# Three reorderings in a six-layer fp32 transformer kernel: pooled low halves, a row sum, and the turn for rotary keys

## The chip, the cores and the metric

The kernel runs on one core of a Trainium2 chip. The metric is the device time of one execution in microseconds; the figure for the kernel before is the median of three runs. Positions in the trace ("at 263 us") count from the first instruction of the profiled execution.

## What is computed

One sequence of 512 tokens with 1024 features passes through a pool mixer, a gated convolution, a latent attention with 16 heads, a second pool mixer, and then two layers that each hold a mixed attention and a feed-forward part. All is float32. The parts that the change touches:

```python
# pool mixer: u, z = split(xn @ w_in); 4 groups g with window w = 2, 4, 8, 16
mean = (c - prev) / min(count, w)          # trailing mean of u, c = cumsum(u)
pooled = mean - u
mixed = (pooled @ w_grp[g]) * scale
x = x + (mixed * silu(z)) @ w_out
# latent attention, per head
q, kv = rms_norm(q_lat) @ w_q_up, rms_norm(kv_lat) @ w_kv_up
p = softmax((q_nope @ k_nope + rope(q_rope) @ k_rope) * scale, causal)
o = p @ v;  x = x + (o * silu(z)) @ w_out
# feed-forward
h = rms_norm(x);  x = x + square(relu(h @ w_ff1)) @ w_ff2
```

## The kernel before

Activations lie transposed in SBUF: 8 tiles x[m] of 128 features by 512 tokens. Every float32 operand of a product is split into a high half (rounded to fp32r) and a low half (the rest), and a product is three matmuls: high by high, high by low, low by high (`mm3`, lines 401 to 404). All weights come in units of up to 128 by 1024, in one fixed order. A unit passes through four hands: SyncE loads it into one of 4 raw buffers, ScalarE writes its high half wh (line 875), VectorE (line 1448) or GpSimd (line 2173) writes its low half wl, and TensorE multiplies it, as a rule with 8 tiles of activations, so 24 matmuls (`xgemm`, `gemm8`). There are only 3 wh and 3 wl buffers. `taking(unit)` on an engine stands for "make the halves of all units up to this one plus two".

The normalisation is not applied to x before the product. The squares of x are summed while the products run already (ScalarE squares, GpSimd adds into acc, line 2182), TensorE sums acc over the partitions by a product with ones (`sum_squares`, line 428), ScalarE takes the root (906), VectorE the reciprocal (1464), and the results of the products are multiplied by it when they are taken out of PSUM (`scaled`, line 1474, or line 2121 in the feed-forward part).

Each engine has a queue written out by hand, which it works through in order. The places that matter:

- `pool_layer` (TensorE 449, ScalarE 954, VectorE 1513). A group g has four u tiles, four z tiles, two units of the group's product. VectorE works on a u tile like this: low half of the weight unit two ahead, take the product out of PSUM (1474), g+1 shifted adds (1530), mean minus token (1535), two fixes of the first columns (1537, 1540), and then the low half of the pooled tile into G (`low`, 1456), which needs the high half. ScalarE has in its queue, for each u tile: high half of the pooled tile (884), then the high half of the next weight unit (875).
- `mla_layer`, the latent attention (TensorE 502 on, ScalarE 1025 on, VectorE 1658 on, GpSimd 2234 on). Even heads bring the rotary part for themselves and the next head: ScalarE copies it with its rows swapped, VectorE multiplies by cos (1614), GpSimd multiplies the swapped copy by sin (2189) and adds (2192, the tile t1; this is `turn`), ScalarE takes the high halves (1035, 1036), VectorE the low halves (1677, 1678), and TensorE uses them in the rotary part of the scores (550). GpSimd also scales the exponentials of each head to probabilities in four instructions (`probs`, 2240), which TensorE transposes behind the next head's scores (490).
- `second_layer`, the feed-forward part: `first_pair` runs the first two weight units, then `sum_squares`, then the units from the third on; ScalarE, VectorE and GpSimd have relu, square and both halves of their results in their queues behind the root. PSUM banks are handed out from a ring (`bank`).

Of the kernel before, what the change touches and what calls it, by code (L numbers as in the profile page):

```python
# [275 lines left out]
def program(nc, D, out):  # L276
    ctx = ExitStack()
    with ctx:
# [101 lines left out]
        def pe_program(handle, c):  # L380
# [36 lines left out]
            def xgemm(st, *key, first=False):  # L417
                gemm8(key, XH, XL, (lambda k: ("xl", st, k)) if first else None)
# [5 lines left out]
            def sum_squares(use):  # L424
                b = bank("rs", use)
                pe.wait_ge(*at(*last_square(use)))
                pe.wait_ge(*at("const"))
                pe.do.matmul(b[:, :], ones, ACC[:, :], start=True, stop=True).then_inc(  # L428
                    *mark("group", ("mm", "rs", use), ("accfree", use)))
# [203 lines left out]
            def second_layer(l):  # L633
# [165 lines left out]
                wo(1, 3, (3,)), wo(1, 5), wo(1, 7), wo(1, 6)  # L799
                first_pair()  # L800
                ring[0] = [home[i] for i in LAST_BANKS]
                sum_squares(st + 1)
                for qd in range(4):
                    for i in range(2 if qd == 0 else 0, 8):
                        xgemm(st + 1, "f1", l, qd, i)
                    if l == 1 and qd == 3:
                        last_proj()
                    else:
                        out_proj(f"f2{l}", qd)
# [46 lines left out]
        def act_program(handle, c):  # L856
# [21 lines left out]
            def taking(*key):  # L878
                weights(unit[key] + LOOK)
# [145 lines left out]
            def mla_layer(done):  # L1025
# [4 lines left out]
                def rope_high(h):  # L1030
                    t = temp("t1", "m", h)
                    act.wait_ge(*at("t1", "m", h))
                    if h:
                        act.wait_ge(*at("mm", "sc", h - 1, 34))
                    act.do.activation(RQ[0][0:64, :], t[0:64, :], ACT.Copy)
                    act.do.activation(RQ[1][64:128, :], t[64:128, :], ACT.Copy).then_inc(*mark("act", ("rqh", h)))
# [47 lines left out]
                high(KRH[:, :], temp("t1", "m", "kr"), ("t1", "m", "kr"), ("rqh", "kr"))  # L1084
                taking("mz", 0)
                rope_high(0)
                silu(0)
                taking("ke", 0)
                k_high(0)
                for h in range(15):  # L1090
                    if h:
                        turned(h - 1)
# [330 lines left out]
        def dve_program(handle, c):  # L1423
# [27 lines left out]
            def taking(*key):  # L1451
                weights(unit[key] + LOOK)
# [59 lines left out]

            def pool_layer(j, st, out_st):
                sc_name = f"pool_scale{j}"
                for g in range(4):
                    w = 2 ** (g + 1)
                    for i in range(4):
                        taking("u", j, g, i)
                        if g == 0 and i == 0:
                            recip_root(st, R[:, :])  # L1520
                        key = (j, g, i)
                        U = own_temp(dve, at, "U", *key)
                        scaled(U, st, ("u",) + key)
                        dve.wait_ge(*at("pads"))
                        src, names = ("U",) + key, ("B1", "B2")
                        for d in range(g + 1):
                            dst = (names[d % 2],) + key
                            o = own_temp(dve, at, *dst)
                            dve.wait_ge(*mine())
                            dve.do.tensor_tensor(o, temp(*src), shifted(src, 2 ** d), ALU.add).then_inc(*mark("dve"))  # L1530
                            src = dst
                        other = own_temp(dve, at, names[(g + 1) % 2], *key)
                        s = temp(*src)
                        dve.wait_ge(*mine())
                        dve.do.scalar_tensor_tensor(other, s, 1.0 / w, U, ALU.mult, ALU.subtract).then_inc(*mark("dve"))
                        dve.wait_ge(*mine())
                        dve.do.tensor_tensor(other[:, 0:w], s[:, 0:w], const[:, C_CNT + 16 * g:C_CNT + 16 * g + w],
                                             ALU.mult).then_inc(*mark("dve"))
                        dve.wait_ge(*mine())
                        dve.do.tensor_tensor(other[:, 0:w], other[:, 0:w], U[:, 0:w], ALU.subtract).then_inc(  # L1540
                            *mark("dve", ("pooled",) + key, ("tfree", "U") + key))
                        k = (g % 2) * 8 + i
                        low(G[k + 4][:, :], other, G[k][:, :], ("gh",) + key, ("gl",) + key, ("tfree", "B1") + key,
                            ("tfree", "B2") + key)
                    for i in range(4):
                        taking("z", j, g, i)
                        scaled(PZ[i], st, ("z", j, g, i), ("zr", j, g, i))
                    for i2 in range(2):
                        taking("grp", j, g, i2)
                        for i in (2 * i2, 2 * i2 + 1):  # L1550
                            key = (j, g, i)
                            t = own_temp(dve, at, "gy", *key)
                            dve.wait_ge(*at("mm", "grp", *key))
                            dve.wait_ge(*at("zs", *key))
                            dve.do.scalar_tensor_tensor(t, ps("grp", *key)[:, :], vcol(sc_name, 4 * g + i), PZ[i],
                                                        ALU.mult, ALU.mult).then_inc(
                                *mark("dve", ("gy",) + key, ("psfree", "grp") + key))
                            yi = (g % 2) * 4 + i
                            low(YL[yi][:, :], t, YH[yi][:, :], ("yh", f"po{j}", g // 2, yi),
                                ("yl", f"po{j}", g // 2, yi), ("tfree", "gy") + key)  # L1560
                    if g % 2:
                        out_proj(f"po{j}", g // 2, out_st if g == 3 else None)
# [95 lines left out]
            def mla_layer():  # L1658
# [75 lines left out]
                q_low(0)  # L1734
                low(KRL[:, :], temp("t1", "m", "kr"), KRH[:, :], ("rqh", "kr"), ("rql", "kr"), ("tfree", "t1", "m", "kr"))
                taking("mz", 0)
                gate(0)
                rope_low(0)
                taking("ke", 0)
                k_low(0)  # L1740
                for h in range(15):
                    scores(h)
                    if h:
# [404 lines left out]
        def pool_program(handle, c):  # L2148
# [85 lines left out]
            def mla_layer():  # L2234
# [19 lines left out]
                for h in range(15):  # L2254
                    if h % 2:
                        taking("qe", h + 1)
                        probs(h)
                        turn(("m", h + 1))
                        taking("ke", h + 1)
                        taking("mz", h + 1)  # L2260
                    else:
                        taking("mz", h + 1)
                        probs(h)
                        taking("qo", h)
                        taking("vk", h)
                    if h == 8:
                        out_proj("mo", 0)
# [299 lines left out]
```

## Time and profile before

| | |
|---|---|
| median of three runs | 2791.34 us (2783.97 to 2792.09) |
| the profiled execution: its time, its span | 2790.05 us, 2788.3 us |
| TensorE (PE) busy | 2719.6 us, 98% of the span |
| VectorE (DVE) busy | 1560.8 us, 56% |
| ScalarE (ACT) busy | 1138.8 us, 41% |
| GpSimd (POOL) busy | 634.2 us, 23% |
| DMA | 238.78 MB, mean 86 GB/s |
| granted TensorE clock, mean | 0.991 |

The profile names a group of instructions by its line, engine and operation and by out<-in. "Idle before" is the time that an engine stood still ahead of an instruction, with what released it. A matmul of 512 columns shows 0.39 us, but starts follow each other closer, as they are pipelined.

### The profile page before, as it was taken

What the parts mean: (1) busy time and instruction counts of PE and PEld (TensorE: products, weight loads), DVE (VectorE), ACT (ScalarE), POOL (GpSimd) and SP (SyncE); (2) the same over time, 40 slices, a digit from 0 to 9 for tenths busy, and PEclk for the clock granted to TensorE, in tenths of its full rate; (3) what the DMA queues carried; (4) which work ended last, traced back from release to release, by engine and by line L of the source; (5) the groups of instructions that cost most, each with busy time, mean ns of one, the idle gap of its engine ahead of it and who ended that gap; (6) DMA issues with size and microseconds to landing.
All of it is one profiled execution on the core that took longest, in us unless ns stands there. A gap on an engine that the chain in (4) does not pass through costs nothing.

```text
span 2788.3 us, 32068 instructions
## 1 busy us (share of the span) xinstructions
PE 2719.6 (98%) x12958; PEld 2271.4 (81%) x12958; DVE 1560.8 (56%) x2306; ACT 1138.8 (41%) x1826; POOL 634.2 (23%) x418
## 2 busy tenths in 40 slices
PE   7999999999989999999999999999999999999998
PEld 6887888888878888888878888778888888788887
DVE  6656555344565646566565768644435668644433
ACT  4313432222345636533225767522224667522222
POOL 1000111011125625400003651411102452411101
PEclk9999999999999999999999999999999999999999
DMA  3222323223221121222222221133333211233231
GB/s 136 98 91 91 101 97 100 98 91 105 92 65 55 58 82 63 76 99 98 91 96 96 76 70 37 61 99 98 95 96 107 76 61 46 61 98 98 92 105 68
DMA packets 68836, 238.78 MB, mean 86 GB/s; under 512 B 7632, under 2 KB 10192, under 8 KB 68688
## 3 DMA queue, kind: packets, MB, share of 16 engines
q1 hardware_dynamic: 68688, 236.73, 26.3%
q8 instruction: 102, 1.67, 0.2%
q14 instruction: 46, 0.38, 0.0%
HBM read 234.60 MB, written 2.10 MB: 85 GB/s over the span
## 4 chain that ended last, share of the span: by engine, by line
PE 84%; DVE 7%; POOL 4%; ACT 3%; issue 1%; DMA 0%; POOLq 0%; SPq 0%; DVEq 0%; ACTq 0%
PE ps L402 27%; PE ps L404 26%; PE ps L403 26%; DVE t L1530 1%; ACT wh L875 1%; POOL s L2240 1%; POOL acc L2182 1%; DVE wl L1448 1%; PE ps L704 1%; PE ps L703 1%; PE ps L490 1%; PE ps L428 1%; POOL wl L2173 1%; DVE xl L1460 1%; DVE t L1474 0%
## 5 line engine op out<-in xcount | busy, mean ns | idle before, releaser
L402 PE MATMUL ps<-xh,wh 128*128 128x512 f32 x1936 | 766.0, 396 | 19.4 <-DVE wl L1448 10.8
L404 PE MATMUL ps<-xh,wl 128*128 128x512 f32 x1936 | 756.9, 391 | 0.0
L403 PE MATMUL ps<-xl,wh 128*128 128x512 f32 x1936 | 756.9, 391 | 0.0
L875 ACT ACTIVATE wh<-raw 128x1024 fp32r<-128x1024 f32 (+2 forms) x453 | 463.5, 1024 | 448.0 <-PE ps L404 447.5
L1448 DVE TENSOR_TENSOR wl<-raw,wh 128x1024 fp32r<-128x1024 f32 (+1 forms) x337 | 412.3, 1224 | 150.8 <-ACT wh L875 150.8
L402 PE MATMUL ps<-yh,wh 128*128 128x512 f32 x1152 | 450.0, 391 | 1.9 <-DVE wl L1448 1.6
L402 PEld LDWEIGHTS ps<-xh,wh 128*128 128x128 f32 x1936 | 365.6, 189 | 104.5 <-DVE wl L1448 20.9
L403 PE MATMUL ps<-yl,wh 128*128 128x512 f32 x1152 | 448.3, 389 | 0.0
L404 PE MATMUL ps<-yh,wl 128*128 128x512 f32 x1152 | 448.3, 389 | 0.0
L403 PEld LDWEIGHTS ps<-xl,wh 128*128 128x128 f32 x1936 | 365.9, 189 | 77.9 <-issue 3.2
L404 PEld LDWEIGHTS ps<-xh,wl 128*128 128x128 f32 x1936 | 365.4, 189 | 77.0
L2173 POOL TENSOR_TENSOR wl<-raw,wh 128x1024 fp32r<-128x1024 f32 (+3 forms) x116 | 258.4, 2237 | 428.1 <-ACT wh L875 427.9
L2182 POOL TENSOR_TENSOR acc<-acc,t 128x512 f32<-128x512 f32 x66 | 89.5, 1356 | 794.7 <-ACT t L896 792.7
L1482 DVE TENSOR_TENSOR x<-ps,x 128x512 f32<-128x512 f32 x160 | 109.9, 689 | 276.5 <-PE ps L404 276.5
L402 PEld LDWEIGHTS ps<-yh,wh 128*128 128x128 f32 x1152 | 216.3, 188 | 47.6 <-DVE wl L1448 2.0
L404 PEld LDWEIGHTS ps<-yh,wl 128*128 128x128 f32 x1152 | 216.2, 188 | 45.2
L403 PEld LDWEIGHTS ps<-yl,wh 128*128 128x128 f32 x1152 | 216.3, 188 | 44.2
L884 ACT ACTIVATE yh<-t 128x512 fp32r<-128x512 f32 x148 | 93.2, 631 | 365.4 <-POOL t L2356 252.2
L1456 DVE TENSOR_TENSOR yl<-t,yh 128x512 fp32r<-128x512 f32 x148 | 122.2, 827 | 193.2 <-ACT yh L884 193.2
L2356 POOL TENSOR_TENSOR t<-t 128x512 f32<-128x512 f32 x64 | 66.7, 1042 | 531.7 <-DVE t L2121 531.7
L1460 DVE SCALAR_TENSOR_TENSOR xl<-x,vec,xh 128x512 fp32r<-128x512 f32 x64 | 88.7, 1403 | 63.9 <-ACT xh L886 63.9
L884 ACT ACTIVATE g<-t 128x512 fp32r<-128x512 f32 x45 | 28.3, 628 | 179.0 <-DVE t L1540 175.3
(233 smaller groups left out, 3547.7 us busy)
## 6 DMA issues: line engine op xcount, KB each, us to landing
raw<-in_ff SPq DMA_DIRECT2D x128, 512.0 KB, 3.6
raw<-in_pool_in SPq DMA_DIRECT2D x64, 512.0 KB, 3.3
raw<-in_conv_in SPq DMA_DIRECT2D x64, 512.0 KB, 3.2
raw<-in_pool_out SPq DMA_DIRECT2D x32, 512.0 KB, 3.2
raw<-in_qk SPq DMA_DIRECT2D x32, 512.0 KB, 3.6
raw<-in_pool_grp SPq DMA_DIRECT2D x16, 512.0 KB, 3.3
raw<-in_conv_out SPq DMA_DIRECT2D x16, 512.0 KB, 3.3
raw<-in_mla_z SPq DMA_DIRECT2D x16, 512.0 KB, 3.5
```

The source lines that it names most:

```text
L402: pe.do.matmul(o, lh, rh_, start=start, stop=False)
L403: pe.do.matmul(o, lh, rl_, start=False, stop=False)
L404: return pe.do.matmul(o, ll, rh_, start=False, stop=stop)
L875: act.do.activation(h[:, 0:ncol], r[:, 0:ncol], ACT.Copy).then_inc(*mark("whi", ("whi", k)))
L884: act.do.activation(dst, src, ACT.Copy).then_inc(*mark("act", done))
L1448: dve.do.tensor_tensor(lo[:, 0:ncol], r[:, 0:ncol], f(h[:, 0:ncol]), ALU.subtract).then_inc(*mark("wlo", ("wlo", k)))
L1456: dve.do.tensor_tensor(dst, src, f(h), ALU.subtract).then_inc(*mark("dve", *done))
L1460: dve.do.scalar_tensor_tensor(dst, src, scale, f(h), ALU.mult, ALU.subtract).then_inc(*mark("dve", *done))
L1482: dve.do.tensor_tensor(x[m][:, :], ps(*key)[:, :], x[m][:, :], ALU.add).then_inc(*mark("dve", ("psfree",) + key, *done))
L2173: pool.do.tensor_tensor(lo[:, 0:ncol], r[:, 0:ncol], f(h[:, 0:ncol]), ALU.subtract).then_inc(*mark("wlop", ("wlo", k)))
L2182: pool.do.tensor_tensor(ACC[:, :], ACC[:, :], temp("sq", use, k), ALU.add).then_inc(*mark("pool", ("acc", use, k), ("tfree", "sq", use, k)))
L2356: pool.do.tensor_tensor(t, t, t, ALU.mult).then_inc(*mark("pool", ("ffs",) + key))
```

## The change

1. VectorE, pool mixer: the low half of the pooled tile i is no longer taken at the end of its own tile but in the next tile, between `scaled` and the shifted adds; that of the fourth tile comes behind `scaled` of the first z tile. ScalarE's queue there is the same as before.
2. TensorE, feed-forward part of both later layers: `sum_squares` stands behind the third weight unit rather than ahead of it. With it the two swap their PSUM banks.
3. Latent attention. GpSimd, odd heads: `turn` and the low half of the weight unit that `taking("ke")` stands for come ahead of `probs`. ScalarE and VectorE, before the first head: the high and low half of the first keys come ahead of the gate's silu and scaling.

```diff
@@ second_layer, TensorE @@
                 first_pair()
                 ring[0] = [home[i] for i in LAST_BANKS]
-                sum_squares(st + 1)
                 for qd in range(4):
                     for i in range(2 if qd == 0 else 0, 8):
                         xgemm(st + 1, "f1", l, qd, i)
+                        if qd == 0 and i == 2:
+                            sum_squares(st + 1)
@@ mla_layer, ScalarE @@
                 rope_high(0)
+                k_high(0)
+                taking("ke", 0)
                 silu(0)
-                taking("ke", 0)
-                k_high(0)
@@ pool_layer, VectorE @@
+                def pooled_low(g, i, src):
+                    key, k = (j, g, i), (g % 2) * 8 + i
+                    low(G[k + 4][:, :], src, G[k][:, :], ("gh",) + key, ("gl",) + key, ("tfree", "B1") + key,
+                        ("tfree", "B2") + key)
...
                         scaled(U, st, ("u",) + key)
+                        if i:
+                            pooled_low(g, i - 1, last)
                         dve.wait_ge(*at("pads"))
...
-                        k = (g % 2) * 8 + i
-                        low(G[k + 4][:, :], other, G[k][:, :], ("gh",) + key, ("gl",) + key, ("tfree", "B1") + key,
-                            ("tfree", "B2") + key)
+                        last = other
                     for i in range(4):
                         taking("z", j, g, i)
                         scaled(PZ[i], st, ("z", j, g, i), ("zr", j, g, i))
+                        if i == 0:
+                            pooled_low(g, 3, last)
@@ mla_layer, VectorE @@
                 taking("mz", 0)
+                rope_low(0)
+                k_low(0)
                 gate(0)
-                rope_low(0)
                 taking("ke", 0)
-                k_low(0)
@@ mla_layer, GpSimd @@
                     if h % 2:
                         taking("qe", h + 1)
-                        probs(h)
                         turn(("m", h + 1))
                         taking("ke", h + 1)
+                        probs(h)
                         taking("mz", h + 1)
```

## Rows read from the trace of the kernel before

**Rows 1.** Waits of TensorE: us in total, times, longest us.
```profile
PE ps L402 <- DVE wl L1448: 12.4, 11, 1.9
PE ps L550 <- DVE g L1678: 8.2, 7, 1.2
```

**Rows 2.** Timeline, DVE, a u tile of g = 3: start, us, [idle before].
```profile
259.94 0.17 DVE L1540 TENSOR_TENSOR t<-t 128x16 f32<-128x16 f32 x1
260.81 0.69 DVE L1456 TENSOR_TENSOR g<-t,g 128x512 fp32r<-128x512 f32 x1 [0.70 <-ACT g L884]
261.76 1.23 DVE L1448 TENSOR_TENSOR wl<-raw,wh 128x1024 fp32r<-128x1024 f32 x1 [0.26 <-ACT wh L875]
```

**Rows 3.** Timeline, DVE, outputs of two units in a row in an output projection.
```profile
157.68 0.69 DVE L1482 TENSOR_TENSOR x<-ps,x 128x512 f32<-128x512 f32 x1 [3.06 <-PE ps L404]
...
163.12 0.69 DVE L1482 TENSOR_TENSOR x<-ps,x 128x512 f32<-128x512 f32 x1 [3.06 <-PE ps L404]
```

**Rows 4.** Timeline, PE, first matmuls of units in g = 2 and g = 3.
```profile
212.50 0.50 PE L402 MATMUL ps<-xh,wh 128*128 128x512 f32 x1 [0.46 <-DVE wl L1448]
...
263.04 0.50 PE L402 MATMUL ps<-xh,wh 128*128 128x512 f32 x1 [1.28 <-DVE wl L1448]
...
270.64 0.50 PE L402 MATMUL ps<-xh,wh 128*128 128x512 f32 x1 [1.84 <-DVE wl L1448]
```

**Rows 5.** Timeline, PE and DVE, g = 0: the fourth u unit, and a wl three units later.
```profile
43.07 0.50 PE L402 MATMUL ps<-xh,wh 128*128 128x512 f32 x1 [0.30 <-DVE wl L1448]
...
57.97 1.23 DVE L1448 TENSOR_TENSOR wl<-raw,wh 128x1024 fp32r<-128x1024 f32 x1 [0.26 <-ACT wh L875]
```

**Rows 6.** Timeline, POOL, odd head 1.
```profile
853.23 2.41 POOL L2173 TENSOR_TENSOR wl<-raw,wh 128x1024 fp32r<-128x1024 f32 x1 [8.52 <-ACT wh L875]
855.62 4.28 POOL L2240 TENSOR_SCALAR s<-s,small 128x128 f32<-128x128 f32 x4
...
862.56 3.81 POOL L2173 TENSOR_TENSOR wl<-raw,wh 128x1024 fp32r<-128x1024 f32 x2
```

**Rows 7.** Timeline, DVE, same head.
```profile
857.72 0.69 DVE L1614 TENSOR_TENSOR t<-ps,cos 128x512 f32<-128x512 f32 x1 [2.33 <-ACT t L1008]
...
863.94 1.57 DVE L1677 TENSOR_TENSOR g<-t,g 64x512 fp32r<-64x512 f32 x1 [3.54 <-ACT g L1036]
865.52 1.39 DVE L1678 TENSOR_TENSOR g<-t,g 64x512 fp32r<-64x512 f32 x1
866.94 0.69 DVE L1474 TENSOR_TENSOR s<-ps,r 128x512 f32<-128x512 f32 x1
867.55 0.68 DVE L1709 TENSOR_TENSOR t<-ps,s 128x512 f32<-128x512 f32 x1
868.93 0.69 DVE L1456 TENSOR_TENSOR yl<-t,yh 128x512 fp32r<-128x512 f32 x1 [0.70 <-ACT yh L884]
```

**Rows 8.** Timeline, PE: first transposition of head 1's probabilities.
```profile
868.70 0.27 PE L490 MATMUL ps<-const,s 128*128 128x128 f32 x1
```

**Rows 9.** Timeline, DVE and PE, before the first head.
```profile
825.93 1.97 DVE L1677 TENSOR_TENSOR g<-t,g 64x512 fp32r<-64x512 f32 x1 [0.19 <-ACT g L1036]
...
829.56 0.77 PE L402 MATMUL ps<-g 128*128 128x512 f32 x1 [5.20 <-DVE g L1456]
```

**Rows 10.** Timeline, PE and ACT, feed-forward start of the first later layer.
```profile
1801.10 2.08 PE L428 MATMUL ps<-acc,const 128*128 128x512 f32 x2 [4.36 <-POOL acc L2182]
...
1803.26 1.28 ACT L906 ACT_TABLE_LOAD   x1 [6.25 <-PE ps L428]
...
1816.62 0.50 PE L402 MATMUL ps<-xh,wh 128*128 128x512 f32 x1 [1.89 <-DVE wl L1448]
```

**Rows 11.** Windows: from:to, length, busy of PE, PEld, DVE, ACT, POOL, granted clock, DMA.
```profile
829.50:835.00 5.50, 5.44 (x19) 5.18 (x20) 0.69 (x4) 1.27 (x1) 1.82 (x1) 0.50 0.62 188
1818.10:1821.40 3.30, 3.30 (x9) 2.57 (x8) 2.17 (x3) 1.58 (x2) 0.18 (x1) 0.50 0.34 132
2446.60:2449.50 2.90, 2.90 (x13) 2.41 (x14) 1.08 (x2) 1.22 (x2) 1.04 (x1) 1.00 0.54 177
```

## The prediction

> **What bounds the kernel now.** First the page: TensorE is busy 98% of the span, so the other engines matter only where TensorE waits for them. Then the list of its waits [rows 1]: the two heads shown are low halves of weight units that VectorE delivers late (12.4 us) and the rotary low half in seven heads (8.2 us); two more waits appear in the timelines, 5.20 us before the first head of latent attention [rows 9] and 4.36 us at the feed-forward row sum [rows 10]. The change aims at such gaps, so what counts is what ends each of them and what is queued behind it. A unit of 24 matmuls takes 5.44 us at full clock: in an output projection VectorE takes one product each 163.12 - 157.68 us, waiting for TensorE both times [rows 3].
>
> **Pooled low halves: +10.5 us.** In group g = 3 the unit starts at 263.04 and 270.64 each had to wait for a wl [rows 4], 7.60 us apart, against 5.44 us of work: the engines that prepare set the pace, and each tile's lateness reaches TensorE in full once its lead is used up. What is on that chain? After the last fix of a tile ends at 260.11, VectorE waits 0.70 us for ScalarE's high half g, takes the low half from 260.81 to 261.50, waits 0.26 us more, and starts wl at 261.76, released by ScalarE's wh [rows 2]. ScalarE's queue holds g first and wh behind it, and g needs the finished tile. So the 1.65 us from 260.11 to 261.76 belong to ScalarE, and the low half lies inside them for nothing. Moved away, it leaves an idle VectorE there; wl starts no earlier. Put in between `scaled` and the adds, it stands on the chain: VectorE is not waiting there. It costs one slot of a 128x512 operation, 867.55 - 866.94 = 0.61 us [rows 7], say 0.60, in each tile but the first. The fourth low half falls behind `scaled` of the first z tile, where VectorE waits for ScalarE again, and costs nothing.
>
> So the wl's of the first, second and third z unit, made in the course of these tiles, come 0.6, 1.2 and 1.8 us later; the second and third are those at 263.04 and 270.64, the third is the last to bind, and TensorE is 3 x 0.60 = 1.8 us later from there on. In the z tiles the chain is shorter than 5.44 us, so the lateness is not given back and not increased: a group costs 1.8 us less its slack at that unit. By group:
> - g = 3: it waits already, slack 0, +1.8 us.
> - g = 2: it waits too (0.46 us at 212.50) [rows 4], slack 0, +1.8 us.
> - g = 1: each tile has one add less, 0.73 us; over four tiles the 0.5 us of g = 2 become a slack of about 2.4 us. More than 1.8: nothing.
> - g = 0: TensorE starts its fourth u unit at 43.07, late; three units on it needs a wl at 43.07 + 3 x 5.44 = 59.39, and that one is there at 57.97 + 1.23 = 59.20 [rows 5]. Its late start has used up the lead of a group that is otherwise fast. With 0.05 us to react the slack is 0.15, so 1.8 - 0.15 = 1.65 us.
>
> A layer: 1.65 + 0 + 1.8 + 1.8 = 5.25 us, two layers 10.5 us. The ends: were `scaled` and low half to overlap fully the cost would be 0; with 0.69 us for a slot it is 12. I take 0.61 as the only row of two such operations back to back. No DMA and no other queue moves; GpSimd is idle there.
>
> **Row sum one unit later: +2.4 us.** Before, TensorE stands 4.36 us until 1801.10 and 1.89 us until 1816.62 [rows 10]. The unit that now goes first has its halves and fills the first gap. But the second gap is released by a wl that stands in VectorE's queue behind the reciprocal and two feed-forward tiles, which all need the row sum; ScalarE's wh of that unit is behind two of its high halves as well. What does the sum itself do? The third unit runs from about 1796.6 to 1802.0, then come the two passes at full clock, about 1.1 us, and ScalarE's root can begin at 1803.15 in place of 1803.26. So the fifth unit starts some 0.1 us earlier, and the 4.4 us filled come out again ahead of it: the fourth unit ends at 1808.8, and TensorE stands until 1816.5, about 7.7 us in one piece. Twice, this gains 0.2 us. And one long gap has a price: after the 5.20 us of [rows 9] the granted clock was 0.50, which is 1.2 of 2.4 GHz, for the next 5.5 us [rows 11], which loses half of that, 2.7 us. The gaps of before cost less behind the fifth unit's start: 0.50 for 3.3 us in the first later layer, and 1.00 in the second [rows 11], 1.65 us together. With 3.3 to 5.5 us at half speed in each layer the cost is 3.3 to 5.5, middle 4.3, less 1.65, less 0.2: +2.4 us, ends +1.4 and +3.6, and -0.2 if no stretch at half clock follows.
>
> **Turn ahead of probabilities: -3.1 us.** In head 1 the turn waits for `probs` to end at 855.62 + 4.28 = 859.90 [rows 6]; its input, the swapped copy, is there at 857.7 [rows 7]. So it moves up by 2.2 us, line 1677 is issued at 861.75 instead of 863.94, and TensorE's wait of 1.2 us [rows 1] goes. What is late next is `probs`, pushed behind turn (2.66 us) and one wl (2.41 us) [rows 6]: wl ends at 862.8, four instructions on their own end at 862.8 + 4.28 = 867.1. Without the wait TensorE asks for them at 868.70 - 1.2 = 867.5 [rows 8]. That would fit. But VectorE and GpSimd are not independent here: lines 1677 and 1678 took 1.57 and 1.39 us beside the wl's of GpSimd [rows 6, 7], where a 128x512 operation takes 0.69, and the second wl, of 384 columns, came out at the end of them. Each such meeting with lines 1677 and 1678 delays `probs` by about 0.4 us, since they take 0.55 us of the shared turn and the instruction had begun: 867.9. The low half of y is issued 2.0 us behind line 1678 [rows 7], hence at 866.35, just as the fourth instruction of `probs` begins; if it gets in first, 0.6 us more: 868.5. So the transposition starts at 867.95 or 868.55 in place of 868.70, 0.75 or 0.15 us gained, in seven heads 5.2 or 1.0. I take the middle, 3.1; the ends are 0 and 8.2.
>
> The Trainium skill ("SBUF — State Buffer", Who interferes with whom) states that a VectorE instruction with two SBUF inputs and a GpSimd instruction that reads SBUF exclude each other, whoever issues first holding the ports for its whole length. The 1.57 us of [rows 7] agree. By its rule the fourth instruction, which begins 0.03 us ahead of the low half of y, would win, and the part would be -5.2 rather than -3.1.
>
> **First keys ahead of the gate: +0.4 us.** ScalarE's k_high comes 1.8 us earlier, but VectorE's k_low stands behind lines 1677 and 1678, and 1677 took 1.97 us beside a wl of GpSimd [rows 9]. It ends at 827.9 as before. And now ScalarE's next wh is earlier too, so GpSimd has its wl of 384 columns waiting when 1677 ends, and 1678 meets it as in head 1: 1.39 us, not 0.69. k_low ends near 829.9 where it ended at 829.5. Ends: -0.3 without that meeting, +0.5. The gate's tile and silu, moved behind, have 5 us until exponentials are due.
>
> **Sum.** 10.5 + 2.4 - 3.1 + 0.4 = +10.2 us on the profiled execution's 2790.05, so 2800.2. The median of the three runs lies 1.3 us higher; carried to it: 2801.5. About 0.3% (8.4 us) is what a measurement of this kernel can tell from no change.
>
> **The rivals.**
> - *Attention gives all it can.* `probs` ends before 867.5 in spite of the meetings: -8.2 instead of -3.1, in sum +5.1, 2796.6 us. For it: the GpSimd instructions are short. Against: 1.57 and 1.39.
> - *More stretches at half clock.* The z units of g = 3 then wait 2.6 and 2.0 us, the one of g = 2 about 2.0 where it was 0.5. Each stretch like that of 1818.10 [rows 11] costs 1.65; with two to three more, +14 to +15, 2806 us. Against: a stretch ahead of another wait for VectorE is absorbed in it.
> - *Faster: the tile's cycle gets shorter.* If wh does not have to wait for g, the 0.70 + 0.26 us of idle VectorE per tile [rows 2] go and the low half only fills: the cycle falls from 7.60 to 6.6 us, and the waits of the low weight halves, 7.2 us of them in the two pool layers, vanish, with half-clock stretches of some 3 us. With the rest of the sum, 2.4 - 3.1 + 0.4 = -0.3, that is about -10.3: 2781 us. It decides where ScalarE's wh would start before the tile is finished. Against it: the row's releaser, wh 1.65 us behind the tile, and a ScalarE queue that the change leaves alone.
> - *The lows cost nothing*, but nothing is gained either: 2791 us.
>
> **How the numbers follow.** My forecast 0.60, attention in full 0.14, more half clock 0.13, faster 0.06, lows free 0.07. Of the forecast's own range (+6 to +13.5) a fifth lies under 8.4 us: slower 0.48 + 0.13 = 0.61, same 0.12 + 0.14 + 0.07 = 0.33, faster 0.06. The range leaves out faster and half of lows free: 2793 to 2809.
>
> **What would show it.** In the profile after: in g = 2 and 3 an idle VectorE of about 1.65 us before each u tile's wl, and 8.2 us between the wl's in g = 3; waits for wl at TensorE up from 12.4 to some 22 us. A wait of 7 to 8 us ahead of the fifth feed-forward unit, with wl as its releaser, and hardly one at the sum. Line 550 without a wait, line 490 with one of 0.4 to 1.1 us on GpSimd in seven heads. Before the first head still 5.5 us. I am wrong if wh starts ahead of g, if the fifth unit starts more than 1 us earlier, or if no wait appears at line 490.

## The result, and the profile after

| | before | after |
|---|---|---|
| median of seven runs each, same chip | 2790.20 us (2783.97 to 2792.29) | 2798.18 us (2796.05 to 2799.39) |
| ratio, 95% interval | | 1.0035 [1.0026, 1.0044] |
| profiled execution: time, span | 2790.05 us, 2788.3 us | 2797.78 us, 2796.0 us |

The kernel became slower by 0.35%, 9.8 us (0.0035 x 2790). The forecast was +10.2 us, so the sign, the size and the range held. The profiled executions, both at a mean granted clock of 0.991, lie 7.7 us apart. How much of the forecast is understanding shows only part by part. The lines named below moved: one further for ScalarE's and VectorE's helpers (wl is now line 1449, the low half 1457, `scaled` 1475), nine further for GpSimd's (wl 2182, `probs` 2249) and for VectorE's rotary lines (1686, 1687).

TensorE's waits in the profile after (us in total, times, longest us), to be held against [rows 1]:

```profile
PE ps L402 <- DVE wl L1449: 31.6, 19, 7.2
...
PE ps L402 <- DVE g L1457: 5.8, 1, 5.8
...
PE ps L490 <- POOL s L2249: 5.4, 7, 0.8
```

Late low halves of weight units cost 31.6 us where they cost 12.4. Of the 31.6, 14.4 are two waits of 7.2 us, one in each feed-forward part, where before had 3.1 us; the other 17.2 stand against 9.3 us of before, and all that is new in them is in the pool mixers, 15.6 us against 7.7. The wait at line 550 (8.2 us in seven heads) is gone, and one at line 490 on GpSimd's probabilities has come, 5.4 us in the same seven heads.

Since the order of TensorE's work hardly changed, the two traces can be laid side by side by the number of the matmul, and the lag of one against the other read at each stage (a later start than in the kernel before counts as positive). That reading is worked out from the starts of all matmuls and has no row of its own. It is taken where the lag has settled, behind any stretch at half clock:

| stage | lag gained there | forecast |
|---|---|---|
| start-up, up to the first units | -1.2 us | 0 |
| pool mixer 1: g = 0, 1, 2, 3 | +1.6, 0, +1.8, +1.8 | +1.65, 0, +1.8, +1.8 |
| before the first head | +0.2 | +0.4 |
| seven odd heads | 7 x -0.38 = -2.7 | -3.1 |
| pool mixer 2: g = 0, 1, 2, 3 | +1.6, 0, +1.8, +1.8 | +1.65, 0, +1.8, +1.8 |
| a stretch at half clock near 1699 us of before, absent after | -0.6 | 0 |
| feed-forward, first and second later layer | +1.1, +1.3 | +2.4 together |
| end | -0.8 | 0 |
| total | +7.7 (as the spans) | +10.2 |

So every part has the forecast sign, and none misses by more than 0.5 us; the stages that the change touches add up to +10.3. The 2.5 us between +7.7 and +10.2 are start-up, end and the missing stretch near 1699 us, which the change does not touch. The timed +9.8 lies nearer to the forecast than the profiled pair, and part of that is the clock: all seven executions of the kernel after have a mean granted clock of 0.991, while those of the kernel before in the experiments below range from 0.991 (2788.7 to 2793.5 us) to 0.994 (2783.5 to 2786.3 us).

### The profile page after: what moved, and what is told of

Same layout as the page of the kernel before. It is cut to its first block, busy times and chain, and to the rows that moved or that the text cites. A ratio compares the mean times of both kernels' runs of the same rounds, so it can differ in the third digit from the quotient of the medians.

```text
span 2796.0 us, 32057 instructions
## 1 busy us (share of the span) xinstructions
PE 2717.7 (97%) x12958; PEld 2265.6 (81%) x12958; DVE 1554.6 (56%) x2306; ACT 1141.2 (41%) x1826; POOL 639.1 (23%) x418
## 4 chain that ended last, share of the span: by engine, by line
PE 84%; DVE 7%; ACT 4%; POOL 3%; issue 1%; DMA 0%; SPq 0%; POOLq 0%; DVEq 0%; ACTq 0%
PE ps L402 27%; PE ps L403 26%; PE ps L404 26%; POOL s L2249 1%; ACT wh L876 1%; DVE t L1539 1%; DVE wl L1449 1%; ACT t L1009 1%; PE ps L490 1%; PE ps L704 1%; PE ps L703 1%; DVE g L1457 1%; POOL wl L2182 1%; PE ps L428 1%; DVE t L1475 1%
```

## The experiments

Each kernel was timed beside the kernel before on one chip; ratios carry a 95% interval, and us are the ratio's distance from 1 times some 2787 us.

### Theory and rivals

The theory is that of the prediction: four independent parts; the low halves used to lie inside VectorE's idle time behind ScalarE's queue and now lie on the chain; the row sum turns a pair of gaps into one long gap; `turn` ahead of `probs` trades one wait for a shorter one. The rivals are that the loss comes from granted clock and not from the moved work, that the pool part costs also where there is slack, and that ScalarE's order, not VectorE's load, is what holds the pool layers.

### Each part alone

Only the pooled low halves (part 1 of the diff).

> Only the pooled low halves are moved, the rest is as before. My theory (the low half lay for nothing inside VectorE's wait for ScalarE's wh, and now stands on the chain): TensorE loses about 1.5, 0, 1.9 and 1.8 us in the groups g = 0 to 3 of each pool layer, 10.4 us in all, ratio near 1.0037; VectorE is idle 1.65 us ahead of each u tile's wl. Rival (the lows cost nothing and the loss of the change comes from elsewhere): no step in TensorE's times in the pool layers, ratio 1.000.

Measured: 1.0042 [1.003, 1.0055], +11.7 us. TensorE's wait for wl in this kernel (lines as in before):

```profile
PE ps L402 <- DVE wl L1448: 17.4, 19, 2.5
```

From 12.4 to 17.4 us, and at the start of the last late unit of each group the matmul-by-matmul lag has stepped by 1.6, 0, 1.8 and 1.8 us, in both layers: 10.4 us. Not all of it stays in this execution. Its half-clock stretch comes one unit earlier than in before, between the two waits of g = 3 (from:to, length, busy of PE, PEld, DVE, ACT, POOL, granted clock, DMA share, GB/s):

```profile
266.80:270.10 3.30, 3.30 (x8) 2.62 (x9) 3.13 (x5) 0.00 (x0) 0.00 (x0) 0.50 0.49 159
```

There the second wait swallows it (0.87 us are left of the 2.46 of the kernel after), while the stretch of before lies behind that unit and costs 1.6 us. Settled, g = 3 therefore costs 0.2 us here, and the two layers 7.2 us. The spans differ by 8.8 us, 3.1 us of which come from one more half-clock stretch near 1752 us of before (last section). So the timed +11.7 is not the moved instruction alone: all five executions have a mean granted clock of 0.991, the 21 of the kernel before have a median of 0.993, and beside those of them at 0.991 (2789.0 to 2791.7 us) this kernel (2797.6 to 2799.3 us) is some 8 us slower. By this estimate the rival of the granted clock holds for 3 to 4 us of the timed figure; the steps show the rest. This part carries the loss of the whole change.

Only the row sum (part 2).

> Only the feed-forward row sum is moved behind the third unit. My theory (the fifth unit's wl hangs on the sum, so the filled gap comes out again, in one piece, and is followed by more time at half clock): a wait of about 7.2 us ahead of the fifth unit in both layers, that unit starts within 0.3 us of where it did, and TensorE is 0.5 to 2 us later behind it in each layer: +1 to +4 us, ratio 1.0004 to 1.0014. Rival (the filled gap is a gain that something else in the change hides): -4 us or more in each layer, ratio 0.997 or less.

Measured: 1.0018 [1.0009, 1.0027], +5.0 us with ends of 2.5 and 7.5. Waits, fifth unit, and two windows behind it (columns as above), one in each later layer:

```profile
PE ps L402 <- DVE wl L1449: 23.8, 11, 7.2
```

```profile
1815.13 0.79 PE L402 MATMUL ps<-xh,wh 128*128 128x512 f32 x1 [7.25 <-DVE wl L1449]
```

```profile
1815.20:1820.00 4.80, 4.80 (x12) 3.73 (x13) 2.73 (x4) 1.58 (x2) 1.04 (x1) 0.50 0.38 109
2445.70:2451.00 5.30, 5.30 (x13) 4.14 (x14) 2.93 (x4) 1.58 (x2) 1.26 (x2) 0.50 0.28 99
```

One wait of 7.25 us, and behind it 4.8 and 5.3 us at half clock, where before had 3.3 us and none [rows 11]. By matmuls the part costs 0.5 us in the first layer, which had a half-clock stretch of its own, and 2.6 us in the second. That is 3.1 us, near the forecast (2.4) and inside the timed interval, whose middle is higher. One likely reason is that the stretch of 3.3 us in before is not always there (the profiles of the third and fourth experiment have none at that place), while those of 4.8 and 5.3 us stand behind waits of 7.2 us; the mean granted clock is 0.991 (median of 11 executions) beside 0.993. How much of the 5.0 us that explains was not measured.

Only GpSimd's order in the odd heads (part 3 without the first keys).

> Only GpSimd's turn and one low half are moved ahead of the probabilities in the odd heads. My theory (the wait at the rotary scores goes, and one of 0.76 us at the transpositions takes its place): 0.41 us gained in each of seven heads, -2.9 us, ratio 0.9990. Rival (the waits are exchanged one for one): 0 us, ratio 1.0000.

Measured: 0.9985 [0.9976, 0.9994], -4.2 us; by matmuls -0.39 us in each of seven heads, -2.7 us. The wait at line 550 is gone, and this one has taken its place:

```profile
PE ps L490 <- POOL s L2240: 5.4, 7, 0.8
```

Only the first keys ahead of the gate, one run.

> Only the first keys are put ahead of the gate. My theory (k_low stands behind lines 1677 and 1678 on VectorE, and 1678 now meets a low half on GpSimd): the wait of TensorE before the first head grows from 5.20 to about 5.7 us, line 1678 takes about 1.4 us where it took 0.69. Rival (k_high's turn on ScalarE was what ended last): the wait shrinks by up to 1 us, line 1678 stays at 0.69.

Measured: 2784.88 us in one run, beside a median of 2786.66, no verdict as a time. TensorE's wait, and the second of the two rotary low halves ahead of it (start, us, [idle before]):

```profile
828.97 0.77 PE L402 MATMUL ps<-g 128*128 128x512 f32 x1 [5.78 <-DVE g L1456]
```

```profile
826.76 1.39 DVE L1678 TENSOR_TENSOR g<-t,g 64x512 fp32r<-64x512 f32 x1
```

The wait grew from 5.20 [rows 9] to 5.78 us, and line 1678 takes 1.39 us, as the prediction had it. Of the 0.6 us nothing is left once the half-clock stretch behind the wait is over, since less work falls into it (4.1 us in place of 5.4); in the kernel after 0.2 us are left. The execution was quicker by four half-clock stretches that it lacks: see the last section.

The four parts add up to 11.7 + 5.0 - 4.2 + 0.5 = 13 us where the whole change has 9.8. The intervals (2.5 to 3.5 us to either side on a part) cover the difference. By matmuls the parts repeat what the kernel after shows in the same stages, but for g = 3 and its half-clock stretch; nothing asks for an interaction.

### Is it really the place on the chain?

Low halves moved in group g = 1 alone, in both layers, where the prediction counts 2.4 us of slack. In the other groups each low half stays behind its own tile.

```diff
@@ pool_layer, VectorE, on top of the first part @@
-                        if i:
+                        if i and g == 1:
                             pooled_low(g, i - 1, last)
...
                         last = other
+                        if g != 1:
+                            pooled_low(g, i, last)
...
-                        if i == 0:
+                        if i == 0 and g == 1:
                             pooled_low(g, 3, last)
```

> The pooled low halves are moved as in the change, but in the group g = 1 alone, in both pool layers. My theory (there the lead is about 2.4 us, more than the 1.8 us by which the halves come later): VectorE's cycle grows by 0.6 us a tile, TensorE does not wait, no difference, ratio 0.9990 to 1.0010. Rival (a slot on VectorE costs TensorE its time wherever it stands): +3.6 us, ratio 1.0013.

Measured: 1.0007 [0.9998, 1.0015]: no clear difference, but the interval holds the rival's 1.0013 as well as 1.000, so the time does not decide; the trace does. The wait of TensorE, and VectorE's wl's in g = 1:

```profile
PE ps L402 <- DVE wl L1448: 12.4, 11, 1.9
```

```profile
98.07 1.23 DVE L1448 TENSOR_TENSOR wl<-raw,wh 128x1024 fp32r<-128x1024 f32 x1 [1.65 <-ACT wh L875]
...
104.78 1.22 DVE L1448 TENSOR_TENSOR wl<-raw,wh 128x1024 fp32r<-128x1024 f32 x1 [1.65 <-ACT wh L875]
```

VectorE's cycle here is 6.71 us, 0.60 longer than the 6.11 of before by the same reading, so the instruction moved onto the chain. TensorE's waits for wl are to the tenth those of [rows 1], and the lag against the kernel before does not move in g = 1 of either layer (0.0 us): the chain had the slack. The same edit costs 1.8 us in g = 3 of the kernel after and nothing in g = 1.

### What holds the pool layers: the order in ScalarE's queue

The prediction blamed ScalarE's queue: the high half g, which needs the finished tile, ahead of wh, which does not. Two kernels exchange them, one with the low halves moved, one with VectorE as before.

```diff
@@ pool_layer, ScalarE @@
+                        weights(unit["u", j, g, i] + LOOK + 1)
                         pooled = temp("B2" if g % 2 == 0 else "B1", j, g, i)
                         high(G[(g % 2) * 8 + i][:, :], pooled, ("pooled", j, g, i), ("gh", j, g, i))
```

With the low halves moved:

> The pooled low halves moved as in the change, and in addition ScalarE makes wh of the next weight unit ahead of the pooled tile's high half, in the u tiles of both pool layers. My theory (the low half was free only because VectorE stood waiting for wh behind g; with wh ready at the end of the tile the move is right): no idle VectorE ahead of wl, a cycle of about 6.65 us between the wl's in g = 3 in place of 8.2, TensorE waits under 1 us in g = 3 and not at all in g = 2; against the kernel before -7 to -11 us, ratio 0.996 to 0.9975. Rival (something else, such as the extra slot on VectorE alone, makes the loss): still slower than before, ratio above 1.002.

Measured: 0.9964 [0.9952, 0.9977], -10.0 us. With this edit alone:

> Only ScalarE's order in the u tiles is changed, wh ahead of the pooled tile's high half; the low halves stay at the end of their tile. My theory: VectorE still waits 0.70 us for the high half, only the 0.26 us ahead of wl go; cycle 7.33 us in g = 3, against the kernel before -3 to -5 us, ratio 0.998 to 0.999, so that the move of the low half is worth 4 to 6 us on top in the other kernel. Rival (wh's place alone makes all the gain): the same time as the kernel with both.

Measured: 0.9969 [0.9957, 0.998], -8.6 us, outside what I expected (-3 to -5). VectorE in g = 3, first of the kernel with both, then of the one with ScalarE's order alone (start, us, [idle before]):

```profile
256.63 0.17 DVE L1549 TENSOR_TENSOR t<-t 128x16 f32<-128x16 f32 x1
256.72 1.22 DVE L1449 TENSOR_TENSOR wl<-raw,wh 128x1024 fp32r<-128x1024 f32 x1
257.86 0.68 DVE L1475 TENSOR_TENSOR t<-ps,r 128x512 f32<-128x512 f32 x1
258.46 0.68 DVE L1457 TENSOR_TENSOR g<-t,g 128x512 fp32r<-128x512 f32 x1
...
263.18 1.22 DVE L1449 TENSOR_TENSOR wl<-raw,wh 128x1024 fp32r<-128x1024 f32 x1
```

```profile
251.09 0.69 DVE L1457 TENSOR_TENSOR g<-t,g 128x512 fp32r<-128x512 f32 x1 [0.70 <-ACT g L884]
251.70 1.22 DVE L1449 TENSOR_TENSOR wl<-raw,wh 128x1024 fp32r<-128x1024 f32 x1
...
258.94 1.22 DVE L1449 TENSOR_TENSOR wl<-raw,wh 128x1024 fp32r<-128x1024 f32 x1
```

Cycles of 6.46 and 7.24 us, against 7.60 before and 8.19 in the kernel after. With wh already made, wl follows the last fix of the tile without idle time, and now the moved low half is right: it no longer makes VectorE wait for g. In the order of before it still does, 0.70 us. TensorE's waits for wl fall from 12.4 us in 11 places to:

```profile
PE ps L402 <- DVE wl L1449: 4.7, 3, 1.9
```

with both, and with ScalarE's order alone to:

```profile
PE ps L402 <- DVE wl L1449: 7.7, 7, 1.6
```

By matmuls the pool layers give 8.3 us with ScalarE's order alone and 13.5 with both. In each, 3.2 us are the two half-clock stretches behind the waits of g = 3, one in each layer, which before has and these two have not. So of the moved work there remain 5.1 and 10.3 us: the expectation for ScalarE's order alone left out the clock and nearly held for the rest. The timed intervals of the two kernels overlap, so that the second step pays (5.2 us by matmuls, 4 to 6 expected) rests on the traces.

### The row sum with its cover

The prediction said that the fifth unit waits because its wh and wl stand behind what needs the row sum in both queues. So: the sum behind the third unit as in the change, and in ScalarE and VectorE the next weight units ahead of the root and of the first tiles.

```diff
@@ second layers, ScalarE and VectorE, on top of the second part @@
                         taking("f1", l, qd, i)
+                        if qd == 0 and i < 3:
+                            weights(unit["f1", l, qd, i] + 5)
                         if qd == 0 and i == 0:
```

> The row sum behind the third unit as in the change, and in addition ScalarE and VectorE make the fifth and sixth weight units ahead of the root, the seventh and eighth in the two tiles behind it. My theory (the fifth unit waits only because its halves are queued behind what hangs on the sum): no wait of 7.2 us ahead of the fifth unit, no half clock behind it, TensorE 5 to 9 us earlier in each layer, some of it lost again where the output projection asks for its last tile; ratio 0.994 to 0.9965. Rival (the fifth unit waits for something else, a PSUM bank or a buffer): the wait stays, ratio above 1.000.

Measured: 0.9983 [0.9974, 0.9992], -4.7 us, less than I expected (-10 to -17). The wait of 7.2 us is gone, and no stretch at half clock follows:

```profile
1808.00:1813.00 5.00, 5.00 (x24) 4.14 (x23) 2.79 (x4) 1.58 (x2) 1.04 (x1) 1.00 0.32 126
```

But TensorE's starts show where part of the gain is handed back:

```profile
1803.92 0.50 PE L402 MATMUL ps<-xh,wh 128*128 128x512 f32 x1 [1.18 <-POOL wl L2178]
...
1839.47 0.50 PE L402 MATMUL ps<-yh,wh 128*128 128x512 f32 x1 [2.62 <-DVE yl L1459]
```

Behind the fifth unit TensorE is 8.5 us earlier in the first layer, 1.6 of them the stretch that before has there, and 6.9 us in the second. In the output projection, whose matmuls need the feed-forward tiles' low halves, 3.6 and 5.2 us are lost again: the wait of 2.6 us above comes in both layers, and in the second a stretch at half clock follows it (2466.20 to 2469.60 us). 5.0 and 1.7 us remain. Units of weights can be made ahead, but the tiles themselves cannot start before the row sum. The expectation named this loss and put it far too low.

### Probabilities between turn and the weight unit

In the profile after, the low half of y delays the fourth instruction of `probs` (next section). If `probs` is moved to stand directly behind `turn`, ahead of the weight unit's 2.41 us, it is finished long before either question arises.

```diff
@@ GpSimd, odd heads @@
-                        probs(h)
                         turn(("m", h + 1))
+                        probs(h)
                         taking("ke", h + 1)
```

> Only GpSimd's turn is moved ahead of the probabilities in odd heads, the low half of the weight unit stays behind them. My theory (the probabilities are late by that low half of 2.4 us and by meetings with VectorE): no wait at the rotary scores, none at the transpositions, at most a wait of 0 to 0.5 us for the weight unit behind them: -6 to -9 us, ratio 0.997 to 0.998. Rival (the meetings with VectorE alone make the probabilities late): a wait of 0.5 us or more stays at the transpositions, ratio 0.9985 or more.

Measured: 0.9967 [0.9954, 0.998], -9.2 us, at the far end of what I expected; by matmuls -1.4 us per head, 9.6 in all. In these heads neither line 550 nor line 490 waits. GpSimd, and the low half of y on VectorE, in head 1:

```profile
858.08 4.70 POOL L2240 TENSOR_SCALAR s<-s,small 128x128 f32<-128x128 f32 x4
862.75 3.82 POOL L2173 TENSOR_TENSOR wl<-raw,wh 128x1024 fp32r<-128x1024 f32 x2
```

```profile
863.33 2.37 DVE L1456 TENSOR_TENSOR yl<-t,yh 128x512 fp32r<-128x512 f32 x1 [0.70 <-ACT yh L884]
```

Now it is the low half of y that is slow, 2.37 us beside a wl in place of 0.69, and TensorE does not notice.

### All that was found, together

Low halves are moved with wh ahead of g, `probs` stands behind `turn`, the row sum has its units ahead, and the first keys are where they were:

> Four edits together: pooled low halves moved with wh ahead of the high half, turn ahead of the probabilities with the low half of the weight unit behind them, the row sum behind the third unit with the weight units ahead. Each took its own wait away, in other stages, so my theory adds them: -10 to -12 in the pool layers, -9 in latent attention, -5 to -7 in the feed-forward parts, -24 to -28 us in all, ratio 0.990 to 0.992. Rival (a gain is lost again at a wait of a later stage): ratio 0.993 or more, with a new wait at TensorE above 2 us in some stage.

Measured: 0.9905 [0.9893, 0.9918], -26.5 us (2761.94 us beside 2787.07). Two of the rival's waits above 2 us are there, those of the output projections, but they are the ones of the row sum's own experiment and take nothing more. What is left of the waits spoken of here:

```profile
PE ps L402 <- DVE yl L1460: 5.2, 2, 2.6
PE ps L402 <- POOL wl L2187: 2.4, 2, 1.2
PE ps L402 <- DVE wl L1452: 2.2, 3, 1.6
```

Without the row sum's edits:

> The same without any edit at the feed-forward row sum. My theory: -19 to -21 us against the kernel before, ratio 0.9925 to 0.9935, so that the row sum's edit with the weight units ahead is worth 5 to 7 us beside it. Rival (that edit is worth nothing beside the others): the same time as the kernel with it.

Measured: 0.9926 [0.9914, 0.9938], -20.6 us. So the two better forms of the pool and attention parts (-10.0 and -9.2 alone) add up, and the row sum with its units ahead is worth about 6 us more. The change contained three moves that pay in a better setting: for the low halves and the row sum it left out what has to move with them, and the turn it put ahead together with a weight unit that should have stayed behind.

## Why the prediction held, point by point

**Pooled low halves: right in mechanism, place and size.** VectorE in g = 3 in the profile after, to be held against [rows 2]:

```profile
256.99 1.23 DVE L1449 TENSOR_TENSOR wl<-raw,wh 128x1024 fp32r<-128x1024 f32 x1 [1.65 <-ACT wh L876]
258.13 0.68 DVE L1475 TENSOR_TENSOR t<-ps,r 128x512 f32<-128x512 f32 x1
258.74 0.68 DVE L1457 TENSOR_TENSOR g<-t,g 128x512 fp32r<-128x512 f32 x1
259.52 2.87 DVE L1539 TENSOR_TENSOR t<-t 128x512 f32<-128x512 f32 x4
...
265.18 1.23 DVE L1449 TENSOR_TENSOR wl<-raw,wh 128x1024 fp32r<-128x1024 f32 x1 [1.64 <-ACT wh L876]
```

The low half now follows `scaled`, which waits for nothing, in a slot of 0.61 us; the idle time ahead of wl is 1.65 us in one piece; the cycle is 265.18 - 256.99 = 8.19 us for a forecast of 8.2. ScalarE shows the reason:

```profile
263.57 0.63 ACT L885 ACTIVATE g<-t 128x512 fp32r<-128x512 f32 x1 [6.61 <-DVE t L1549]
264.11 1.04 ACT L876 ACTIVATE wh<-raw 128x1024 fp32r<-128x1024 f32 x1
```

It stands idle for 6.61 us with a wh to make, since g is ahead of it and waits for the tile. At TensorE, [rows 4] have these answers:

```profile
214.70 0.50 PE L402 MATMUL ps<-xh,wh 128*128 128x512 f32 x1 [1.68 <-DVE wl L1449]
...
274.65 0.50 PE L402 MATMUL ps<-xh,wh 128*128 128x512 f32 x1 [2.46 <-DVE wl L1449]
```

0.46 became 1.68, and 1.84 became 2.46; TensorE's lag came out at 1.8 us in g = 2 and in g = 3. The bolder statements held too: 1.6 us in g = 0, where the unit at 43.07 [rows 5] had used up the lead (forecast 1.65), and nothing in g = 1, which was then shown alone. The waits for wl add up to 31.6 us, where the prediction said "from 12.4 to some 22": it left out its own two waits of 7 to 8 us. Nor does a sum of waits give the lag: in the pool mixers it grew by 7.9 us and the lag by 10.4, since a short wait shows less than it costs (the unit at 47.84 in the profile after waits 0.23 us, and TensorE's lag grows by 0.53 us there). The forecast of the time was not made from that figure.

**Row sum: right, and the forecast wait was there.** TensorE in the first later layer:

```profile
1822.63 0.79 PE L402 MATMUL ps<-xh,wh 128*128 128x512 f32 x1 [7.23 <-DVE wl L1449]
```

with VectorE's and ScalarE's part in it,

```profile
1811.30 3.35 DVE L1465 RECIPROCAL r<-t 128x512 f32<-128x512 f32 x1 [10.91 <-ACT t L907]
...
1821.35 1.22 DVE L1449 TENSOR_TENSOR wl<-raw,wh 128x1024 fp32r<-128x1024 f32 x1 [0.26 <-ACT wh L876]
```

```profile
1820.28 1.04 ACT L876 ACTIVATE wh<-raw 128x1024 fp32r<-128x1024 f32 x1
```

and half clock behind it:

```profile
1822.30:1828.40 6.10, 5.77 (x14) 4.51 (x15) 3.40 (x5) 1.58 (x2) 1.59 (x2) 0.50 0.32 97
```

Forecast were 7.7 us of wait and 3.3 to 5.5 us at 1.2 GHz in each layer; there are 7.23 us of wait in both, and about 6 us at half clock in the first layer and 3 in the second. Before, ScalarE's table load behind the sum began at 1803.26 [rows 10]; the one of after begins at 1809.28. That is 6.0 us later, and TensorE was 6.2 us later by then from the parts ahead: the sum itself gained 0.1 us, as forecast. The lag grew by 1.1 and 1.3 us, 2.4 for a forecast of 2.4, although the clock's share fell otherwise on the two layers than assumed: that the sum comes out to the tenth is chance. The first layer paid less than its 6 us at half clock suggest, since it had a stretch of its own before [rows 11]. One end of the prediction is summed wrongly: without any stretch at half clock behind the fifth unit the part would be -1.65 - 0.2 = -1.85 us, not -0.2.

**Turn ahead of probabilities: right in size, half by chance.** Forecast: -3.1; measured: -2.7, with line 490 as the new wait. VectorE and GpSimd in head 1 of the profile after:

```profile
866.02 1.57 DVE L1686 TENSOR_TENSOR g<-t,g 64x512 fp32r<-64x512 f32 x1 [1.38 <-ACT g L1037]
867.60 0.77 DVE L1687 TENSOR_TENSOR g<-t,g 64x512 fp32r<-64x512 f32 x1
...
870.39 0.70 DVE L1457 TENSOR_TENSOR yl<-t,yh 128x512 fp32r<-128x512 f32 x1 [0.70 <-ACT yh L885]
```

```profile
864.63 2.41 POOL L2182 TENSOR_TENSOR wl<-raw,wh 128x1024 fp32r<-128x1024 f32 x1
867.01 5.43 POOL L2249 TENSOR_SCALAR s<-s,small 128x128 f32<-128x128 f32 x4
872.41 1.00 POOL L2182 TENSOR_TENSOR wl<-raw,wh 128x384 fp32r<-128x384 f32 x1
```

The four instructions of `probs`, 4.28 us on their own [rows 6], take 5.43 beside VectorE: the meetings are there. (The view names the four by the shape of the first; they have 128, 256, 384 and 512 columns, and the last takes 1.57 us alone.) But line 1687 took 0.77 us and not the 1.39 of its twin in [rows 7], and the undecided case fell to VectorE: the low half of y at 870.39 has its 0.70 us undisturbed, while the fourth instruction of `probs`, which by its record begins 0.02 us earlier, takes 2.07 in place of 1.57, in all seven heads. I had taken the middle between the two outcomes (0.15 and 0.75 us a head), and the measured 0.38 lies near it, although only one of them took place: it was the worse one, and the meetings cost the four instructions 1.15 us where the prediction had counted 1.4. A mean of two cases is no mechanism, and here it was right by luck.

The rule of the Trainium skill that the prediction set against it ("SBUF — State Buffer", Who interferes with whom: whoever issues first holds the ports for its whole length) gave -5.2 us by the order of the records, and -2.7 were measured. The exclusion it describes agrees, 2.07 us for an instruction that takes 1.57 alone; the order of two records 0.02 us apart does not say who is first.

**First keys: right.** 5.77 us before the first head, where 5.20 stood [rows 9]:

```profile
834.13 0.77 PE L402 MATMUL ps<-g 128*128 128x512 f32 x1 [5.77 <-DVE g L1457]
```

with line 1687 at 1.39 us, the meeting with GpSimd's wl of 384 columns that the prediction described. The lag at this matmul grew by 0.6 us for a forecast of 0.4, and 0.2 are left behind the stretch at half clock.

**The rivals.** Attention in full (-8.2) did not happen, and the experiment with `probs` directly behind `turn`, which is another order, gained 9.2 us without either wait. More half clock did not show in the pool layers of the profiled pair, which has one stretch in each layer on either side; it shows in the timed figures, by some 2 us on the whole change (9.8 against 7.7) and not by the 4 to 5 of the rival. The faster rival named wh ahead of g as the deciding point and about -10 us as the price; ScalarE's queue was as the prediction said, so it did not come about, and the kernel that makes it true gained 10.0 us. Of what would have proved the prediction wrong (wh ahead of g, the fifth unit over 1 us earlier, no wait at line 490) none was seen.

## What to carry to other kernels

Before moving an instruction out of a place where its engine waits, ask what that engine waits for next. If it is another engine's in-order queue, the instruction was free; moved, it costs its whole slot wherever the chain has no slack (1.8 us in g = 3, nothing in g = 1). The gain lies in the releaser's queue: put there what needs nothing (the next weights) ahead of what must wait (the high half of an unfinished tile), and only then fill the other engine. A reduction moved later needs the work behind it prepared ahead of it in every queue, or the gap comes back in one piece and at half clock; and its own consumers come later, which takes a part back.

## What the runs showed of the hardware

The granted clock behind short gaps differs between executions with the same code at the place. Windows at one place of pool mixer 1, of the kernel before, and then of the kernel with only the first keys moved, whose code is the same up to there (columns as in [rows 11]):

```profile
271.90:275.10 3.20, 3.20 (x9) 2.47 (x8) 1.83 (x2) 1.31 (x2) 0.00 (x0) 0.50 0.47 165
```

```profile
271.00:274.50 3.50, 3.42 (x15) 2.81 (x16) 1.85 (x4) 1.58 (x2) 0.00 (x0) 1.00 0.47 154
...
1814.00:1817.40 3.40, 3.40 (x17) 2.80 (x16) 1.67 (x2) 1.58 (x2) 0.78 (x1) 1.00 0.55 154
```

Behind the same gap of about 1.9 us one execution runs 3.2 us at 1.2 GHz and the other none; the last row is the same pair for the place of 1818.10 in [rows 11]. The kernel before had five such places in its profiled execution (near 272, 811, 1446, 1699 and 1818 us) where the one with the first keys moved had one, near 811. By matmuls the stretches near 272, 1446 and 1818 cost 1.6 us each and the one near 1699 0.6 us; the one near 811 costs nothing, as TensorE waits 5.20 us behind it in any case [rows 9].

A longer one stands at another place, behind a gap of 1.35 us that both kernels have: first the kernel before, then the one with the low halves moved in g = 1 alone, whose code there is the same.

```profile
1752.90:1759.70 6.80, 6.80 (x37) 5.64 (x36) 4.73 (x9) 5.12 (x13) 0.00 (x0) 1.00 0.02 8
```

```profile
1751.80:1758.60 6.80, 6.80 (x23) 5.67 (x22) 3.83 (x7) 4.59 (x12) 0.00 (x0) 0.50 0.01 2
```

It costs 3.1 us, and the executions with only the low halves moved and with all edits together have it too. Behind the gaps of 5 to 7 us before the first head and, in the change, before the fifth unit it came every time. So two profiled spans can differ by some 5 us for reasons outside a change, as much as three of the four parts here, and timed runs as well: 17 executions of the kernel before on one chip take 2783.5 to 2786.3 us at a mean granted clock of 0.994 and 2790.0 to 2793.5 us at 0.991. The lag by stage tells the parts apart where the span does not, if it is read behind such stretches and they are matched.

Why the short gaps differ is open; no experiment was aimed at it. Open too is what decides between a VectorE and a GpSimd instruction that begin within 0.03 us of each other.
